# Three layer-norm joints: the first tile through the norm alone, and three slabs multiplied tile by tile

## The reference, cut to what matters

```python
def layer_norm(x, g, b):
    xf = x.astype(jnp.float32)
    mu = xf.mean(-1, keepdims=True)
    var = jnp.square(xf - mu).mean(-1, keepdims=True)
    return ((xf - mu) * lax.rsqrt(var + LN_EPS) * g + b).astype(x.dtype)

for layer in range(DEPTH):
    ...
    h = layer_norm(DN_ALPHA * h + mix.astype(h.dtype), ln_g[layer, 0], ln_b[layer, 0])
    ffn = peer(h, peer_w_q[layer], peer_sub_keys[layer], peer_u[layer], peer_v[layer])
    h = layer_norm(DN_ALPHA * h + ffn.astype(h.dtype), ln_g[layer, 1], ln_b[layer, 1])

def mixer_c(x, w_in, lower_bound, norm_g, w_out):
    h = x @ w_in
    ...
def peer(x, w_q, sub_keys, u_tab, v_tab):
    ...
        q = (xt @ w_q).reshape(T, PEER_HEADS, 2, PEER_HALF)
```

## Time and profile before

| | us |
|---|---|
| median of 3 runs (2913.05 to 2915.61) | 2913.15 |
| the profiled execution's own time | 2912.49 |
| its span | 2910.7 |
| PE busy in the span | 2868.4 (99%) |
| DVE, ACT, POOL busy | 1940.5, 1566.0, 896.2 |

### The profile page before, as it was taken

The page is one execution under the profiler, slowest core; times in us unless marked ns, Lnnn a source line. Parts: engine busy times, 40 slices in busy tenths (PEclk is TensorE's granted clock), DMA queues, the critical chain, the costliest instruction groups (busy, mean ns, idle before and its releaser), DMA issues.

```text
span 2910.7 us, 59696 instructions
## 1 busy us (share of the span) xinstructions
PE 2868.4 (99%) x21515; PEld 2619.3 (90%) x21515; DVE 1940.5 (67%) x3380; ACT 1566.0 (54%) x2559; POOL 896.2 (31%) x361
## 2 busy tenths in 40 slices
PE   8999999999999999999999999999999999999999
PEld 7899999888888889999988888789799999988887
DVE  4388577787556537947778855675539667788655
ACT  4444444676545554444467744654544544577554
POOL 3689600000004368960000000255779810000000
PEclk9999999999999999999999999999999999999999
DMA  6455555555754455565555575433465555555654
GB/s 218 158 184 184 184 168 171 174 174 178 237 193 159 146 164 183 181 187 169 172 174 175 178 233 196 139 130 123 162 190 183 181 177 170 169 178 174 208 192 161
DMA packets 146464, 515.20 MB, mean 177 GB/s; under 512 B 17552, under 2 KB 18576, under 8 KB 146336
## 3 DMA queue, kind: packets, MB, share of 16 engines
q1 hardware_dynamic: 146336, 513.46, 54.3%
HBM read 509.20 MB, written 4.19 MB: 176 GB/s over the span
## 4 chain that ended last, share of the span: by engine, by line
PE 91%; DVE 3%; POOL 2%; issue 2%; ACT 2%; DMA 0%; SPq 0%; DVEq 0%; ACTq 0%; POOLq 0%
PE col L576 15%; PE col L578 15%; PE col L577 15%; PE acc L576 13%; PE acc L578 13%; PE acc L577 13%; POOL w_lo L527 2%; PE col L723 2%; PE acc L723 2%; PE acc L683 1%; DVE work L2486 0%; ACT work L889 0%; ACT w_hi L829 0%; PE acc L2297 0%; PE misc L2310 0%
## 5 line engine op out<-in xcount | busy, mean ns | idle before, releaser
L527 POOL TENSOR_TENSOR w_lo<-ring,w_hi 128x1024 fp32r<-128x1024 f32 x357 | 896.0, 2520 | 1448.3 <-ACT w_hi L829 1447.3
L829 ACT ACTIVATE w_hi<-ring 128x1024 fp32r<-128x1024 f32 x941 | 993.9, 1056 | 529.1 <-PE acc L578 447.2
L576 PE MATMUL col<-x_hi,w_hi 128*128 128x256 f32 (+1 forms) x3976 | 1125.9, 283 | 6.8 <-DVE x_lo L1089 5.5
L577 PE MATMUL col<-x_lo,w_hi 128*128 128x256 f32 (+1 forms) x3976 | 1119.6, 282 | 0.0
L578 PE MATMUL col<-x_hi,w_lo 128*128 128x256 f32 (+1 forms) x3976 | 1119.1, 281 | 0.0
L527 DVE TENSOR_TENSOR w_lo<-ring,w_hi 128x1024 fp32r<-128x1024 f32 x584 | 714.1, 1223 | 378.6 <-ACT w_hi L829 375.6
L576 PEld LDWEIGHTS col<-x_hi,w_hi 128*128 128x128 f32 x3976 | 751.4, 189 | 11.1 <-issue 6.7
L578 PEld LDWEIGHTS col<-x_hi,w_lo 128*128 128x128 f32 x3976 | 752.4, 189 | 0.0
L577 PEld LDWEIGHTS col<-x_lo,w_hi 128*128 128x128 f32 x3976 | 748.3, 188 | 0.7
L576 PE MATMUL acc<-w_hi,c_hi 128*128 128x512 f32 x1664 | 654.5, 393 | 3.1 <-POOL w_lo L527 2.1
L578 PE MATMUL acc<-w_hi,c_lo 128*128 128x512 f32 x1664 | 648.8, 390 | 0.0
(11 more groups left out here) (300 smaller groups left out, 1873.9 us busy)
## 6 DMA issues: line engine op xcount, KB each, us to landing
ring<-in_u SPq DMA_DIRECT2D x384, 512.0 KB, 3.6
ring<-in_v SPq DMA_DIRECT2D x384, 512.0 KB, 3.6
ring<-in_wq SPq DMA_DIRECT2D x48, 512.0 KB, 3.6
ring<-in_s_in SPq DMA_DIRECT2D x21, 512.0 KB, 3.2
ring<-in_c_in SPq DMA_DIRECT2D x16, 512.0 KB, 3.6
ring<-in_s_out SPq DMA_DIRECT2D x16, 512.0 KB, 3.2
ring<-in_s_gate SPq DMA_DIRECT2D x12, 512.0 KB, 3.2
ring<-in_s_conv SPq DMA_DIRECT2D x12, 512.0 KB, 3.2
```

Source lines behind the costliest of these rows:

```text
L527: eng.tensor_tensor(k.w_lo[s.slot][:, :], k.ring[s.slot][:, :], k.w_hi[s.slot][:, :].bitcast(F32), ALU.subtract).then_inc(k.lo[s.slot], 1)
L576: pe.matmul(out, a[0], b[0], start=start, stop=False, **kw)
L577: pe.matmul(out, a[0], b[1], start=False, stop=False, **kw)
L829: act.activation(k.w_hi[s.slot][:, :], k.ring[s.slot][:, :], ACT.Copy).then_inc(k.hi[s.slot], 1)
```

## The change

The list `TILE_FIRST` names the stages that are opened in the new way: peer0, c and peer1. For these, PE's `open_stage` takes the place of `transpose_x` and of the first three `features`: it transposes tile 0, multiplies slab 0 by tile 0 and slab 1 by tile 0, transposes tile 1, multiplies slab 2 by tile 0, and then the three slabs by tile 1. `tile_features` issues 24 matmuls of 128 columns for one slab and one tile, and waits for one `x_ready` before each half of the features where the tile is fresh. Only the pass over tile 1 counts `used`. The filler matmuls become 8, 16 and 6. DVE puts the second half of tile 1's residual and its mean ahead of all centring, takes tile 0's variance, centring, root and scaling first, and writes `x_lo` of tile 0 inside the norm, before the second half of tile 1 is centred. ACT takes the root of tile 0 between the squares of tile 0 and those of tile 1, and puts `w_hi` of the third slab and the root of tile 1 between the roundings of tile 0 and those of tile 1.

```diff
+TILE_FIRST = ("peer0", "c", "peer1")
...
+    def tile_features(self, s, t, fresh):
+
+        k = self.k
+        if t == 0:
+            self.bank_free(s)
+            self.slab_ready(s)
+        hi, lo = slab_view(k, s)
+        cut = slice(t * P, (t + 1) * P)
+        for c in range(DC):
+            if fresh and c % 4 == 0:
+                self.w.next(k.x_ready)
+            ins = self.split_matmuls(k.col[s.slot][:, cut], (hi[:, c, :], lo[:, c, :]),
+                                     (k.x_hi[:, c, cut], k.x_lo[:, c, cut]), c == 0, c == DC - 1)
+        if t:
+            ins.then_inc(k.used, 1)
...
+    def open_stage(self, first, src, parts):
+
+        k = self.k
+        self.keep_busy(8)
+        self.w.next(k.mean, NT)
+        self.keep_busy(16)
+        self.transpose_tile(src, 0, parts)
+        self.keep_busy(6)
+        for n in range(SLOTS):
+            self.tile_features(Slab(first + n), 0, n == 0)
+            if n == 1:
+                self.transpose_tile(src, 1, parts)
+        for n in range(SLOTS):
+            self.tile_features(Slab(first + n), 1, n == 0)
...
-            for t in range(NT):
-                self.centred_squares(t)
-            for t in range(NT):
-                self.tile_std(t, eps)
+            self.centred_squares(0)
+            self.tile_std(0, eps)
+            self.centred_squares(1)
             self.split_lead(Slab(end + 1))
             self.lead_x([0])
+            self.split_lead(Slab(end + 2))
+            self.tile_std(1, eps)
             self.lead_x([1])
-            self.split_lead(Slab(end + 2))
...
+        if not rms_next:
+            residual(1, 1)
+            minus_mean(1)
+            variance(0)
+            centre(0, 0)
+            centre(0, 1)
+            self.inverse_std(0)
+            scale(0, 0)
+            variance(1)
+            scale(0, 1)
+            centre(1, 0)
+            self.rest_x_part(0, 0)
+            self.rest_x_part(0, 1)
+            centre(1, 1)
+            self.inverse_std(1)
+            scale(1, 0)
+            scale(1, 1)
+            self.w.skip(k.h_part, 4)
+            self.rest_x_part(1, 0)
+            self.rest_x_part(1, 1)
+            return
```

More of the change, by code:

```diff
@@ L633, in keep_busy, with transpose_tile @@
             self.pe.matmul(k.col[2][:, 0:2 * P], ones[:, 0:P], ones, start=True, stop=True)
+    def tile_features(self, s, t, fresh):
[12 more added lines that the diff above has]
+            ins.then_inc(k.used, 1)
+    def transpose_tile(self, src, t, parts):
+        k, pe = self.k, self.pe
+        for half in range(2):
+            pe.wait_ge(k.h_part, parts - 4 + 2 * t + half + 1)
+            for c in range(4):
+                ins = pe.transpose(k.acc[t * 2 + half][:, c * P:(c + 1) * P],
+                                   src[t][:, (4 * half + c) * P:(4 * half + c + 1) * P], k.ident[:, :])
+            ins.then_inc(k.xt, 1)
+    def open_stage(self, first, src, parts):
[11 more added lines that the diff above has]
+            self.tile_features(Slab(first + n), 1, n == 0)
     def while_normed(self, before_s):
@@ L685, in scores @@
                 ins.then_inc(k.s_full, 1)
-        for n in range(HP):
+        opened = SLOTS if f"peer{layer}" in TILE_FIRST else 0
+        for n in range(opened, HP):
             self.features(Slab(first + n), fresh=n == 0)
@@ L801, in tensor_program @@
         meta = view(k.big, NORMED + 2 * D, D, p=META) if name == "s" else None
-        e.transpose_x(src, meta, k.parts_before(name), BUSY[name], name in ("peer0", "c", "peer1", "s"))
+        if name in TILE_FIRST:
+            e.open_stage(k.first[f"wq{name[4]}" if name[:4] == "peer" else f"{name}_in"], src, k.parts_before(name))
+        else:
+            e.transpose_x(src, meta, k.parts_before(name), BUSY[name], name == "s")
         if name == "s":
@@ L1093, in rest_x, with rest_x_part @@
         w.skip(k.xhi, 4)
+    def rest_x_part(self, t, half):
+        k = self.k
+        self.w.next(k.xhi)
+        cut = (slice(None), slice(4 * half, 4 * half + 4), slice(t * P, (t + 1) * P))
+        self.dve.tensor_tensor(k.x_lo[cut], k.acc[t * 2 + half][:, :].rearrange("p (c t) -> p c t", c=4),
+                               k.x_hi[cut].bitcast(F32), ALU.subtract).then_inc(k.x_ready, 1)
     def add_residual(self, t, half, last, alpha, sums=False, saved=False):
@@ L1133, in centre @@
         def centre(t, half):
-            self.w.next(k.sq)
+            if rms_next:
+                self.w.next(k.sq)
             dve.wait_ge(k.mean, means + t + 1)
@@ L1140, in variance @@
         def variance(t):
+            if not rms_next:
+                self.w.next(k.sq, 2)
             dve.tensor_scalar(k.small[:, 4 + t:5 + t], k.small[:, 40 + 2 * t:41 + 2 * t],
@@ L1167, in layer_norm @@
         scale(1, 0)
[L1168 to L1177, removed]
+        self.mean_square(0)
+        scale(1, 1)
+        self.rms_norm(0, 2)
+        self.mean_square(1)
+        self.rest_meta()
+        self.rms_norm(1, 2)
     def finish_rms(self, name, last):
@@ L1454, in vector_program @@
     for name in k.stages:
-        e.rest_x(META if name == "s" else 0, lead=Slab(0) if name == k.stages[0] else None)
+        if name not in TILE_FIRST:
+            e.rest_x(META if name == "s" else 0, lead=Slab(0) if name == k.stages[0] else None)
         if name[:4] == "peer":
@@ L1762, in tensor @@
         first = k.first["c_in"]
-        for n in range(16):
-            e.features(Slab(first + n), fresh=n == 0)
+        for n in range(SLOTS, 16):
+            e.features(Slab(first + n))
         def wide(*chunks):
```

## The result

| | before | after |
|---|---|---|
| median of 5 runs, us | 2915.61 (2913.05 to 2918.07) | 2928.37 (2925.43 to 2931.39) |
| ratio to before | | 1.0046, 95% interval 1.0034 to 1.0058 |
| span of the profiled execution, us | 2910.7 | 2928.2 |
| PE busy, us | 2868.4 | 2892.1 |

The change makes the kernel slower by 0.46%, 13.4 us of 2915.6, with 9.9 to 16.9 us in the interval; the two medians lie 12.8 us apart. The time of 2928.4 lies in the range and 2.1 us under the forecast. The forecast of the difference, 17.4 us, was further off than that: it was counted from a median of 2913.15, and the five runs here have 2915.61.

A forecast was written before the change was run, and what follows sets the result against it. PE, busy in 99% of the span, was taken as the bound. Per joint, 2.6 us won, 0.9 for late transposes and 7.5 for narrow matmuls lost: 5.8 longer, 17.4 over three, 2913.15 becoming 2930.5 us; range 2916 to 2941, forecast's own 2923 to 2938.

The forecast's parts named there:

- The price of the narrow products: In each joint, 144 matmuls of 128 columns at 0.111 us replace 72 of 256: 16.0 us for 8.5, giving back 7.5.
- The start of the norm: Tile 0's norm comes earlier, so PE's first product starts at 1052.3 instead of 1054.88: 2.6 us won a joint.
- the mark: Start of the fourth slab in a joint of the kernel before, forecast as 19.86 us behind the first residual addition.
- The covers: In the six passes, `w_lo`, `w_hi`, tile 1's root and `x_lo` are ready before PE wants them; all hidden.
- Rival A: Weight loads hide behind narrow products, 0.065 us a start; fourth slab 0.6 us earlier, 2911.3 us in all; chance 0.10.
- Rival B: A narrow fp32r matmul costs what a plain f32 one does, 0.222 us; 21.8 us a joint, 2978.6; chance 0.08.
- Rival C: The granted clock falls in the joints' narrow products; 2934 to 2982 us; chance 0.06.
- far end: Upper end of Rival C's loss: weight loads slow down too at the lower clock, 16 us more.
- near end: Lower end of Rival C's loss: 128 columns at 1.2 GHz still fit in 0.111 us, 1.3 us for leaving that clock.

The follow-up runs named there:

- e3: The changed kernel with each pass of 128 columns cut into two of 64, 288 matmuls in a joint; one run, 3064.8 us.
- e2: The kernel before, norm and transposes unchanged, each of the three opening slabs multiplied in two passes of 128 columns; ratio 1.0126 (1.0083 to 1.0168).
- e1: The changed kernel's norm order, but both tiles transposed before the first slab and slabs multiplied whole, 72 matmuls of 256 columns; 2924.97 us, ratio 1.0029.
- e6: Joint cut by halves of the features instead of by tiles, chunks 0 to 3 of three slabs first, 256-column matmuls; 2915.84 us, ratio 1.0004.
- e8: e6 with the passes reordered so that slab 0 is finished sooner; 2913.67 us against 2915.63, ratio 0.9995 (0.9986 to 1.0004).
- e4: e2 with passes of 192 and 64 columns, and the filler as pairs of bf16 matmuls of 128 columns; one run, 2949.3 us.
- e7: e1 with 24 filler matmuls instead of 6 between the tiles' transposes and 5 behind the last ones; 2918.51 us, ratio 1.0010 (1.0001 to 1.0019).

## Why the prediction was right

**The price of the narrow products** was the step that decided, and it held: 0.111 us a product forecast, 0.112 measured, 16.13 us for the 144 against 16.0. The reasoning was to look, in a trace without such an instruction, for what stays when the columns go: 24, 64 and 128 columns of plain f32 at 0.10 to 0.12. The experiments with 64 and 192 columns confirm for fp32r that the columns do not matter; that the loaded block is what costs remains an inference.

The load formula of the Trainium skill ("TensorE: Matmul & The Clock Gate", section "LDWEIGHTS (loading the stationary operand)") gives 0.107 us for 128 columns, and the traces agree within 5% at full clock (0.112); at 0.50 they show 0.213, so there the measurement decides. The 81 ns of the Trainium skill (the same page, section "Back-to-back issue gap") for a pair at 128 columns is not what these runs show: 0.112 us with 32-bit weights, 0.056 in the bf16 filler.

**The start of the norm** was mis-sized: 2.6 us forecast, 3.06 to 3.12 measured. The term is the pair of centrings, for which I took 1.57 us from the earlier trace rows. It took 1.41 and the reciprocal began 5.14 us behind the first residual addition, not 5.38. In the kernel before each centring of tile 1 had to wait for ACT's squares (`w.next(k.sq)`), so the row held a wait as well as work. The variance before the second scaling cost less than I gave it too. With the mark at 19.96 that makes the joint 5.3 us longer instead of 5.8, the sum 15.8 instead of 17.4. That the time came within 2.1 us of the forecast owes something to luck: the joints lost 1.6 us less than forecast, the medians differ by 4.6 us less, and the median before, from which the forecast was counted, turned out 2.5 us higher.

**The covers** held: PE waited for no `w_lo` in the six passes, and the fourth slab was ready in time. The loss was carried to the end, as PE is the bound behind it.

**Rival A** (loads hidden) is refuted by 0.112 at 128 columns, and by the same at 64 and 192. **Rival B** (0.222) is refuted in the joints at full clock. **Rival C** did not happen in the changed kernel's joints, PEclk was 1.00 in each. The clock did fall in `e3`, in 64-column products without any wait. I had given it 0.06, and its price in `e3` is what I had put at its far end, a doubled load. My near end, 128 columns that still start every 0.111 at 1.2 GHz, finds no support: 64 and 192 columns took 0.213 there. In `e2` the lower mean clocks of two of the four runs (0.992 and 0.987) may be the same thing in passes of 128 columns; that is not shown.

**Where I was wrong** were expectations: in `e1` I gave PE a wait of 2.3 us and no account of the clock, in `e3` again none of the clock, and in `e6` I left out the wait for the fourth slab's `w_lo`, which took the gain.

## What to carry to other kernels

Before a matmul with 32-bit weights is split into narrower ones, count matmuls, not columns: at the full clock each of 192, 128 or 64 columns costs 0.112 us, against 0.118 for 256, so two halves cost nearly twice the whole. Overlap at a joint is better bought by splitting the contraction (which chunk comes first) than the columns (`e8` has its fourth slab 0.7 to 0.8 us a joint earlier, though its total is not told from that of the kernel before), and then one must see when the slab's buffer is given back. And where a reordering lengthens a wait of TensorE, look at the granted clock behind the wait before you explain the time.

## What the runs showed of the hardware that was not expected

- An fp32r matmul with its own 128x128 weight block starts every 0.111 to 0.112 us at the clock of 1.00, with 64, 128 or 192 columns (`e3`, `e2`, `e4`). At 0.50 it is 0.213, with 64 and with 192.
- In bf16 a load and a matmul of 128 columns take 0.056 us (`e4`).
- The clock fell to 0.50 in a stretch in which PE was never idle (`e3`); before it PE ran 64-column fp32r products. With 128 columns a load, for 16 us, it stayed at 1.00 in the joints of the profiles of the changed kernel and of `e2`; with 192 and 64 in turn it fell in the third slab, about 11 us behind the first product (`e4`).
- In `e1` a wait of 2.27 us, eight transposes and a wait of 0.76 were followed by about 6 us of products at 0.50, 2.6 us lost in all; 24 filler matmuls in the first wait and 5 in the second kept 1.00 (`e7`).
